# One stream over all heads for the prompt's sparse attention, and an earlier first projection chunk: a transformer layer on one Trainium2 core

## The reference

```python
h = rms(x, norm1_g) * (1 + sc1) + sh1
z = h @ w_in                     # q_nsa, new K/V rows, gates, q_dif, ...
...
# for each of 8 heads, queries qn (1024 x 64)
o_c, p_c = sdpa(qn, kc, vc)      # 32 compressed keys: one for 32 tokens
o_s = sdpa(qn, selected blocks of ks, vs)   # causal
o_w = sdpa(qn, kw, vw)           # causal, window of 512
o_a = g0 * o_c + g1 * o_s + g2 * o_w
```

## Time and profile before

| | us |
|---|---|
| runs (3): median, lowest, highest | 2254.08, 2253.2, 2257.63 |
| profiled execution: its own time, its span | 2250.43, 2248.6 |
| PE busy over the span | 2054.2 (91%) |
| DVE, ACT busy | 1148.2 (51%), 629.9 (28%) |
| DMA rate over the span | 74 GB/s |
| sparse attention, first score to last add | about 727.95 to 1051.29 |

### The profile page before, as it was taken

One profiled execution on the slowest core, in us unless ns is written; L12 is line 12 of the kernel. 1 busy time (PEld: TensorE's weight loads), 2 busy tenths in 40 slices (PEclk: granted clock), 3 DMA queues, 4 the chain that ended last, 5 costly groups with the idle time before them and its releaser, 6 DMA issues. The chain is left out here.

```text
span 2248.6 us, 35510 instructions
## 1 busy us (share of the span) xinstructions
PE 2054.2 (91%) x12626; PEld 1829.8 (81%) x12626; DVE 1148.2 (51%) x2510; ACT 629.9 (28%) x1212; POOL 119.0 (5%) x176
## 2 busy tenths in 40 slices
PE   5989999978995999998887969789999999999997
PEld 1338889858995888887667967589999999999996
DVE  0434333323235666766877643545555555555555
ACT  2113334411222555654773011211111011011012
POOL 1031100001300000000102000000000000000000
PEclk9999999988996998998999989889999999999998
DMA  9765545212101000000002351032201211112104
GB/s 316 256 197 176 154 133 176 79 41 82 48 1 61 1 0 0 0 0 0 1 0 86 122 179 56 20 103 57 56 28 56 56 28 56 50 34 56 37 1 151
DMA packets 132511, 166.07 MB, mean 74 GB/s; under 512 B 15851, under 2 KB 98635, under 8 KB 132372
## 3 DMA queue, kind: packets, MB, share of 16 engines
q1 hardware_dynamic: 117790, 134.75, 19.0%
q0 software_dynamic: 4832, 17.15, 2.4%
q10 hardware_dynamic: 9808, 13.11, 1.7%
HBM read 144.31 MB, written 22.77 MB: 74 GB/s over the span
## 5 line engine op out<-in xcount | busy, mean ns | idle before, releaser
L1659 DVE TENSOR_TENSOR late_x<-late_x,ffn_po 128x344 f32<-128x344 f32 x528 | 244.1, 508 | 116.5 <-PE ffn_po L1589 116.3
L1572 PE MATMUL ffn_pg<-late_words_hi,ffn_uhi 128*128 128x344 f32 x528 | 169.3, 321 | 14.6 <-DVE ffn_ulo L1623 14.6
L1533 ACT ACTIVATE ffn_sg<-ffn_pg 128x344 f32<-128x344 f32 x66 | 30.2, 458 | 534.1 <-PE ffn_pg L1572 534.1
L1589 PE MATMUL ffn_po<-ffn_a_hi,ffn_ohi 128*128 128x344 f32 x528 | 169.0, 320 | 0.2 <-DVE late_x L1659 0.2
L1572 PE MATMUL ffn_pg<-late_words_lo,ffn_uhi 128*128 128x344 f32 x528 | 169.1, 320 | 0.0
L1572 PE MATMUL ffn_pg<-late_words_hi,ffn_ulo 128*128 128x344 f32 x528 | 169.1, 320 | 0.0
L1589 PE MATMUL ffn_po<-ffn_a_hi,ffn_olo 128*128 128x344 f32 x528 | 168.9, 320 | 0.0
L1572 PE MATMUL ffn_pv<-late_words_hi,ffn_uhi 128*128 128x344 f32 x528 | 168.8, 320 | 0.0
L1572 PE MATMUL ffn_pv<-late_words_lo,ffn_uhi 128*128 128x344 f32 x528 | 168.7, 319 | 0.0
L1572 PE MATMUL ffn_pv<-late_words_hi,ffn_ulo 128*128 128x344 f32 x528 | 168.7, 319 | 0.0
L1589 PE MATMUL ffn_po<-ffn_a_lo,ffn_ohi 128*128 128x344 f32 x528 | 168.2, 319 | 0.0
(11 more groups left out here) (456 smaller groups left out, 4625.9 us busy)
## 6 DMA issues: line engine op xcount, KB each, us to landing
mod_wr<-in_w_ada SPq DMA_DIRECT2D x12, 2048.0 KB, 9.1
ffn_raw_u<-in_w_ffn_in SPq DMA_DIRECT2D x44, 512.0 KB, 5.7
dec_kin<-in_cache_kv SPq DMA_DIRECT2D x64, 256.0 KB, 3.6
ffn_raw_o<-in_w_ffn_out SPq DMA_DIRECT2D x22, 512.0 KB, 3.8
gate_d<-dec_gate ACTq DMA_DIRECT2D x48, 172.0 KB, 2.3
late_x<-gate_d SPq DMA_DIRECT2D x8, 1032.0 KB, 5.6
dec_raw<-in_w_in POOLq DMA_DIRECT2D x16, 512.0 KB, 5.6
dec_vin<-in_cache_kv SPq DMA_DIRECT2D x64, 128.0 KB, 2.2
```

The lines of the kernel that those rows point to most:

```text
L1533: act.activation(sg[(j + c) % 2][:], pg[(j + c) % 2][:, 0:TCH], ACT.Silu).then_inc(silu_done, 1)
L1572: mm = pe.matmul(bank[b][:, 0:TCH], w[j][:, v * KD + k, :], h[:, k, tok], start=(k == 0 and q == 0), stop=(k == KD - 1 and q == 2))
L1589: mm = pe.matmul(po[u % 4][:, 0:TCH], w[j][:, k * P:(k + 1) * P], a[j][:, tok], start=(q == 0), stop=(q == 2))
L1659: dve.tensor_tensor(total[:, k, tok], total[:, k, tok], po[u % 4][:, 0:TCH], ALU.add).then_inc(o_read, 1)
```

## The change

The attention's loops over heads are gone: all engines walk one written-out list of items over 8 x 16 = 128 units, with constant semaphore thresholds and addresses. The tiles are taken in the order [7, 0, 6, 1, 5, 2, 4, 3]. LAG becomes 3. `qhi` and `qlo` exist twice; the next head's queries are an item in the middle of the current head (in front of its unit 10), and so are the turning of the compressed probabilities ("turned", in front of unit 4) and their product with the values ("blocks", in front of unit 5). These items take turns with the units in the two `sc` slots, by their place in the list. The compressed result is copied into z first, and `finish` adds both branches to it. The tables are halved at the head's start.

The first projection chunk is fetched in the decode stage, once the last pair's keys have been read, and split by DVE at H = 90; the second chunk's fetch is issued behind it. `zraw`, `zhi` and `zlo` lie where `kin` lies, and `od` moves to `early`, a view of `vin`.

```diff
+        raw, hi0, lo0 = g.zraw[:], g.zhi[:], g.zlo[:]
+        whi = [hi0, s.sb("whi1", [P, KD, ZCH], F32R)[:]]
+        wlo = [lo0, s.sb("wlo1", [P, KD, ZCH], F32R)[:]]
...
-                        sp.wait_ge(raw_free, n)
-                    sp.dma_start(raw[:], w[:, :, c * ZCH:(c + 1) * ZCH]).then_inc(w_in, 16)
+                    if n >= 2:
+                        sp.wait_ge(raw_free, n - 1)
+                        sp.dma_start(raw, w[:, :, c * ZCH:(c + 1) * ZCH]).then_inc(w_in, 16)
...
-                    dve.wait_ge(w_in, n * 16 + 16)
                     if n >= 2:
+                        dve.wait_ge(w_in, n * 16 - 16)
                         dve.wait_ge(acc_full, (n - 1) * TT)
-                    dve.tensor_copy(whi[j][:], raw[:]).then_inc(w_hi, 1)
-                    dve.wait_ge(w_hi, n + 1)
-                    dve.tensor_tensor(wlo[j][:], raw[:], f32(whi[j][:]), ALU.subtract).then_inc(w_lo, 1)
-                    dve.wait_ge(w_lo, n + 1)
+                    else:
+                        dve.wait_ge(g.z_next, 16)
+                    dve.tensor_copy(whi[j], raw).then_inc(w_hi, 1)
+                    dve.wait_ge(w_hi, n)
...
-                split(0)
...
+    TILES = [7, 0, 6, 1, 5, 2, 4, 3]
...
+    head_units = [(k, i, 0, 0, (i + 1) * P) if b == 0 else (k, i, 1, max(0, i - 4) * P, (i + 1) * P)
+                  for k, i in enumerate(TILES) for b in range(2)]
+    units = [(h, *x) for h in range(NH) for x in head_units]
+    UT = len(units)
+    LAG = 3
+    Q_AT, T_AT, V_AT = 10, 4, 5
+
+    items = []
+    for u, x in enumerate(units):
+        h, at = x[0], u % NU
+        if u == 0:
+            items.append(("queries", 0))
+        if at == 0:
+            items.append(("compressed", h))
+        if at == T_AT:
+            items.append(("turned", h))
+        if at == V_AT:
+            items.append(("blocks", h))
+        if at == Q_AT and h + 1 < NH:
+            items.append(("queries", h + 1))
+        items.append(("unit", u))
...
+                def transpose_probs(v):
+                    nt = (units[v][5] - units[v][4]) // P
+                    pe.wait_ge(p_full, v + 1)
+                    for gr in range(groups[v]):
+
+                        if gr == 0:
+                            if v:
+                                pe.wait_ge(tp_act, v)
+                        elif second[v]:
+                            pe.wait_ge(tp_dve, second[v])
+                        for q in range(4 * gr, min(nt, 4 * gr + 4)):
+                            mm = pe.transpose(tp[gr][:, (q - 4 * gr) * P:(q - 4 * gr + 1) * P],
+                                              prob[v % 4][:, q * P:(q + 1) * P], g.ident[:])
+                        mm.then_inc(tp_full, 1)
+
+                def values(v):
+                    h, k, i, b, k0, k1 = units[v]
+                    nt = (k1 - k0) // P
+                    if b == 0 and v >= 4:
+                        pe.wait_ge(o_free, v // 2 - 1)
+                    pe.wait_ge(tp_act, v + 1)
+                    for gr in range(groups[v]):
+                        if gr:
+                            pe.wait_ge(tp_dve, second[v] + 1)
+                        for q in range(4 * gr, min(nt, 4 * gr + 4)):
+                            mm = pe.matmul(out[v // 2 % 2][:, b, :], probT[v % 2][:, q, :],
+                                           g.z[:, k0 // P + q, VCOL[b]:VCOL[b] + P], start=(q == 0), stop=(q == nt - 1))
+                    mm.then_inc(pv_done, 1)
+
+                for n, (kind, x) in enumerate(items):
+                    slot = n % 2
+                    if n >= 2:
+                        pe.wait_ge(sc_free, n - 1)
+                    if kind == "queries":
+                        pe.wait_ge(q_dup, 2 * x + 2)
+                        for t in range(TT):
+                            mm = pe.transpose(sc[slot][:, t * P:(t + 1) * P], qd[:, t].rearrange("p a b -> p (a b)"), g.ident[:])
+                        mm.then_inc(q_ps, 1)
+                    if kind == "compressed":
+                        pe.wait_ge(sc_free, place["queries", x] + 1)
+                        for i in range(TT):
+                            mm = score(slot, 32 * i, x, i, 0, 32, g.kkc)
+                        mm.then_inc(sc_full, 1)
+                    if kind == "turned":
+                        pe.wait_ge(c_step, x * NC + NC)
+                        for half in range(2):
+                            mm = pe.transpose(sc[slot][:, half * P:(half + 1) * P],
+                                              scmp[:, 4 * half:4 * half + 4, :].rearrange("p t n -> p (t n)"), g.ident[:])
+                        mm.then_inc(sc_full, 1)
+                    if kind == "blocks":
+                        pe.wait_ge(c_ev, x + 1)
+                        for half in range(2):
+                            mm = pe.matmul(sc[slot][:, half * 4 * HD:(half + 1) * 4 * HD], pcT[:, half, :],
+                                           g.vcb[:].rearrange("p a b -> p (a b)"), start=True, stop=True)
+                        mm.then_inc(sc_full, 1)
+                    if kind == "unit":
+                        h, k, i, b, k0, k1 = units[x]
+                        score(slot, 0, h, i, k0, k1, g.kk[b]).then_inc(sc_full, 1)
+                        if x >= LAG:
+                            transpose_probs(x - LAG)
+                        if x >= LAG + 1:
+                            values(x - LAG - 1)
+                for x in range(UT, UT + LAG + 1):
+                    if x < UT + LAG:
+                        transpose_probs(x - LAG)
+                    values(x - LAG - 1)
...
+                for n, (kind, x) in enumerate(items):
+                    if kind == "queries":
+                        act.wait_ge(q_ps, x + 1)
+                        act.activation(qhi[x % 2][:], sc[n % 2][:], ACT.Copy).then_inc(q_hi, 1)
...
+                    dve.wait_ge(c_add, h + 1)
+                    dve.scalar_tensor_tensor(out=o, in0=out[f % 2][:, 0, 0:HD], scalar=share[:, f % 2, 0:1], in1=o,
+                                             op0=ALU.mult, op1=ALU.add).then_inc(o_step, 1)
+                    dve.wait_ge(o_step, f + 1)
+                    dve.scalar_tensor_tensor(out=o, in0=out[f % 2][:, 1, 0:HD], scalar=share[:, f % 2, 1:2], in1=o,
+                                             op0=ALU.mult, op1=ALU.add).then_inc(o_free, 1)
...
+                for n, (kind, x) in enumerate(items):
+                    at_sc = sc[n % 2]
+                    if kind == "queries":
+                        dve.wait_ge(q_hi, x + 1)
+                        dve.tensor_tensor(qlo[x % 2][:], at_sc[:], f32(qhi[x % 2][:]), ALU.subtract).then_inc(sc_free, 1)
+                    if kind == "compressed":
+                        for t in (g.tcmp, g.tsel, g.twin):
+                            halve_slopes(t)
+                        dve.wait_ge(tab, x * 3 + 3)
+                        dve.wait_ge(sc_full, scored[n])
+                        tn = lambda a: a.rearrange("p (t n) -> p t n", t=TT)
+                        dve.tensor_tensor(scmp[:], tn(at_sc[:, 0:TT * 32]), tn(g.tcmp[:]), ALU.add).then_inc(sc_free, 1)
+                        dve.wait_ge(sc_free, n + 1)
+                    if kind == "turned":
+                        dve.wait_ge(sc_full, scored[n])
+                        dve.tensor_copy(pcT[:].rearrange("p a b -> p (a b)"), at_sc[:, 0:2 * P]).then_inc(c_ev, 1)
+                        dve.wait_ge(c_ev, x + 1)
+                        dve.sem_inc(sc_free, 1)
+                    if kind == "blocks":
+                        dve.wait_ge(sc_full, scored[n])
+                        dve.tensor_copy(g.z[:, 0:TT, C_QN + x * HD:C_QN + (x + 1) * HD],
+                                        at_sc[:, 0:TT * HD].rearrange("p (t d) -> p t d", d=HD)).then_inc(c_add, 1)
+                        dve.wait_ge(c_add, x + 1)
+                        dve.sem_inc(sc_free, 1)
+                    if kind == "unit":
+                        h, k, i, b, k0, k1 = units[x]
+                        w = SEQ if b == 0 else WINDOW + P
+                        table = g.tsel if b == 0 else g.twin
+                        dve.wait_ge(sc_full, scored[n])
+                        if x >= 4:
+                            dve.wait_ge(tp_full, turned_up_to[x - 3])
+                        dve.tensor_tensor_reduce(prob[x % 4][:, 0:k1 - k0], at_sc[:, 0:k1 - k0], table[:, w - (k1 - k0):w], -1.0, 3e38,
+                                                 ALU.add, ALU.min, nmax[:, x % NU:x % NU + 1]).then_inc(biased, 1)
+                        dve.wait_ge(biased, x + 1)
+                        dve.sem_inc(sc_free, 1)
+                        compressed(h, x % NU)
+                        if x >= LAG and groups[x - LAG] == 2:
+                            second_half(x - LAG)
+                        v = x - LAG - 2
+                        if v >= 0 and units[v][3] == 1:
+                            finish(v)
...
```

(20 more changed lines are left out.)

## The result

The median is 2227.18 us (2226.9 to 2227.57, 4 runs) beside 2253.74 for the kernel before (2253.2 to 2257.63, 4 runs): 26.6 us less, a ratio of 0.988, 95% interval [0.987, 0.989]. The forecast was 2233.2, in a range of 2216 to 2249. The profiled execution took 2227.57 (span 2225.8), that of before 2250.43: 22.9 us less. Engines and DMA of the page are almost as before (PE is busy 92% of the span); the written-out heads show in the instruction queues alone, which fetched 64 and 45 packets instead of 48 and 33.

What follows compares the result with a forecast made beforehand. PE was taken as the bound late in each head, with waits and a lower clock at head starts and an idle join. Terms -11.4 and -9.5 (-20.9) on 2250.43 gave 2229.5, 2233.2 for the median; range 2216 to 2249.

Steps and rivals of the forecast that it cites:

- The first chunk: Join of decode stage and projection: fetching and splitting the first weight chunk earlier saves 11.4 us, bounds -12 and -5.
- The attention: All 8 heads at 38.0 us plus first head and tail: 313.8 us against 323.3, so -9.5.
- PE's work: Attention: PE's matmuls and transposes in one head at full clock, 34.8 us, all of which stays.
- (b): In front of unit 10: DVE waits about 2.1 us for `qhi`, so PE waits about 1.5 us at unit 11.
- (a): Start of each head: "turned" and unit 4 wait about 1.7 us for DVE's fourth maximum.
- The first head: Start of the attention: half clock and an empty pipeline add 2.0 us.
- The tail: Behind the attention's last score: transposes, values, latencies, last `finish` and one halving add 7.8 us.
- the 37 under which the forecast called itself wrong: Attention: a head taking under 37 us was named as a sign against the forecast of 38.
- Rival 1: Attention: PE alone is the bound, bubbles shrink to 1.3 us, 36.1 us a head, 2218 in all; chance 0.2.
- Rival 2: Attention: DVE stays the bound, its gaps don't shrink, 39.5 us a head, 2245 in all; chance 0.12.
- Rival 3: Join: the early chunk brings nothing, fetch late or split holding up `outputs`, 2244 in all; chance 0.05.
- Rival 4: Attention: the clock still falls once a head, 2254, chance 0.08; twice a head, 2275, chance 0.05.

Runs made afterwards that it cites:

- queries_at_8: The changed kernel with the next head's query transposes in front of unit 8 instead of unit 10: 2217.83 us, ratio 0.984.
- lag2: The changed kernel with LAG 2 instead of 3, so transposes 2 and values 3 units behind the scores: 2235.5 us, ratio 0.992.
- attn_only: The kernel before with the new attention alone, first chunk fetched and split as before: 2235.16 us, ratio 0.992.
- dve_written_out: The kernel before with the loop over the heads written out on DVE alone: 2239.4 us, ratio 0.994.
- natural order: The changed kernel with its query tiles in the order 0 to 7 instead of long and short in turn: 2216.39 us, ratio 0.983.
- unrolled_old_order: The kernel before with all loops over the heads written out, same order and lag: 2240.72 us, ratio 0.994.
- pe_written_out: The kernel before with the loop over the heads written out on PE alone: 2255.78 us, ratio 1.001.
- chunk_only: The kernel before with the early first chunk alone, attention as it was: 2242.45 us, ratio 0.995.

## Why the prediction was right, and where it was off

**The first chunk** held in each step: fetch at 445.93 (forecast 441.5; the 4.4 us are those of the decode stage), split under DVE's idle time, `outputs` not late, PE 0.55 us behind the stage (forecast 0.6), -11.5 in the trace and -11.4 by itself on the chip. Forecast -11.4.

**The attention** was forecast at 313.8 us and took 304.8. By the terms of a head, 34.8 + 1.7 + 1.5 = 38.0 forecast, 37.09 measured:
- PE's work 34.8: PE was idle for 2.0 of 37.09, so 35.1. Right.
- (b) the queries, 1.5: 1.36. Right in size and place, half right in cause. I had ACT come late, from the exponential of unit 9. In the trace ACT waited 0.44 us for PE's transposes; the way from them over two copies is 2.4 us by itself, and what sets the wait is PE's work under it, about 1.0 us. Asking that question would have shown the remedy that `queries_at_8` then showed.
- (a) the head's start, 1.7: under 0.1. This is the term that failed, and the largest error: 8 x 1.65 = 13 us, in part made up by the waits that follow below. Head start of the changed kernel, timeline:

```profile
844.30 1.06 PE L698 MATMUL nsa_out<-zs_z,nsa_probT 128*128 128x128 f32 x8
...
845.19 0.38 PE L719 MATMUL nsa_sc<-g_ident,nsa_scmp 128*128 128x128 f32 x2
...
845.22 0.28 DVE L852 CUSTOM_DVE_ANT_0 nsa_prob<-nsa_sc,at_twin 128x128 f32<-128x128 f32 x1
845.43 0.08 DVE L852 DVE_READ_ACCUMULATOR2_ANT nsa_nmax<- 128x1 f32 x1
...
845.62 0.50 PE L669 MATMUL nsa_sc<-at_kk,nsa_qhi 128*128 128x512 f32 x1
```

  The head starts at 834.60. DVE ended its fourth maximum 10.9 us behind that, not 11.9, and PE reached "turned" after 10.6 us, not 10.1; unit 4 starts 0.1 us behind the maximum. "Turned" doesn't even wait for the fourth maximum: its slot is that of the third. I had also counted DVE too slow: 33.2 us a head forecast, 30.5 measured (37.09 less 6.6 of waiting for others). In the old order, written out, it lost 3.3 us of gaps a head, not 2.5.
- Not forecast: 0.62 us a head of PE waiting for ACT's copies, and a price for LAG 3. I took it as given that transposes would find their data; `lag2` shows that this is worth 1.4 us a head.
- The first head: +3.2 (40.29 - 37.09) for +2.0; in `attn_only`, with the same code, it was +0.9, so the place of the low clock in that head seems to be worth as much as the term. The tail: +4.9 (41.99 - 37.09) for +7.8; the last head has no queries' item, 0.9 and its wait of 1.36, which I had left in.

Sum of the differences: -7.3 (heads), +1.2, -2.9 = -9.0 us, the error of the attention's term. In the profiled pair it was nearly offset by the 7.9 us in unchanged code, so that the forecast for this execution, 2229.5, lay only 1.9 us off. On medians it is 6.0, and the change gave 26.6 us where 20.9 were forecast. So the range was met with a mechanism that was right except for the head's start; that the end came out closer than its largest term is luck. A head of 37.09 also lay just above the 37 under which the forecast called itself wrong.

**The rivals.** Rival 1 (PE alone bounds, 36.1 a head) has the truth half: the wait at the start is gone, but the queries' is not; its figure is what `queries_at_8` reached, 36.02. Against it speaks that added DVE work still counts by half. Rival 2 fell with the gaps at 0.18 to 0.20 us. Rival 3 fell by the join: neither the fetch nor `outputs` was late. `dve_written_out` puts constants in the place of the waits and addresses that depend on the loop's register, drops the loop's branches and changes nothing else on DVE, and it takes 3.3 us a head out, some 26 us of DVE's time in 8 heads. So the gaps belong to the loop, as the prediction had it; but most of them are the new addresses, and a single wait with a threshold from the register cost nothing that the trace shows. The branch price of the Trainium skill ("Advanced Engine Details and Errata", Control Flow Timing; about 108 ns) makes about 1 us in 8 heads by my estimate, against the 14 us that the run took out of the attention; the passage between two turns of the loop, branch and all, gave 0.25 us a head. Rival 4 fell: the clock is 1.00 from the second head on, also in natural order, with PE idle for 1.35 us at the queries of each head.

## What to carry to other kernels

Compare the distance of two dependent small instructions inside a loop with that in straight code (0.31 against 0.20 us here) and multiply the difference by the number of links that take a new address from the loop's register or stand behind three waits on it: writing out DVE's loop alone gave three quarters as much in the attention as the whole change. When an item goes over several engines before it frees a buffer, count all that the waiting engine has to do meanwhile, with the lagged transposes and values, and put the item where this is longest: moving it by two units gave 1 us a head, and a nicer-looking order of the rest gave nothing. An engine that waits 6.6 of 37 us is not one with 6.6 us to spare: find out by adding work to it.

## What the runs showed of the hardware

The granted clock's low stretches in unchanged code moved between profiles, and with them several us at one place. In the window from 350.80 to 370.00 thirteen profiles have a mean of 0.91 to 0.93, the changed kernel's 0.64, with PE busy 19.20 of 19.20 us as in the kernel before: 4.4 us. `unrolled_old_order`, whose code is the same up to the attention, lost 3.3 us already ahead of that window (its copy of `kcT` stands at 358.63, before at 355.32). `pe_written_out`, whose code is also the same up to there, lost 4.7 us between 180 and 220; PE in that window, first in the kernel before, then in this run:

```profile
180.00:220.00 40.00, 39.19 (x269) 0.96 0.47 155
180.00:220.00 40.00, 39.20 (x238) 0.83 0.47 154
```

The end of the decode stage lies between 501.35 (`attn_only`) and 507.87 us (`pe_written_out`) in the fourteen profiles, and both of these run the old decode stage. The Trainium skill ("TensorE: Matmul & The Clock Gate", Part 1) says that the number of matmuls at the low clock varies from run to run of one kernel. The five runs of `chunk_only` agree: the fastest, 2238.69 us, has a mean clock of 0.951, the slowest, 2244.73, one of 0.948. Whether the long stretch is in each execution of the changed kernel, whose four lie within 0.7 us, is open: one was profiled. A few microseconds between two kernels are to be read from the stage, not from the total.
